# Fourth layer of a four-layer network on one core: retention in pieces beside the input products, outputs and gates by feature

## What is computed

```python
RET_HEADS, RET_DK, RET_DV = 4, 256, 512

def retention_mixer(h, w_in, w_out):
    proj = h @ w_in                                  # 1024 x 6144
    rq, rk, rv, rg = _split(proj, (1024, 1024, 2048, 2048))
    q = rotary(_heads(rq, RET_HEADS), pos)
    k = rotary(_heads(rk, RET_HEADS), pos) * RET_DK ** -0.5
    v = _heads(rv, RET_HEADS)
    o = retention_chunkwise(q, k, v)   # o_t = sum_{s<=t} gamma_h^(t-s) (q_t . k_s) v_s
    o = rms_norm_2(o) * jax.nn.silu(_heads(rg, RET_HEADS))
    return _merge(o) @ w_out                         # 2048 x 1024

x = x + gt_m * retention_mixer(rms_norm_2(x) * (1 + sc_m) + sh_m, ...)
x = x + gt_f * swiglu(rms_norm_2(x) * (1 + sc_f) + sh_f, ...)
```

## Time and profile before

| | before |
|---|---|
| median of 3 runs | 1613.58 us |
| the profiled execution | 1613.15 us |
| its span | 1611.4 us |
| PE, PE weight loads | 94%, 92% of the span |
| DVE, ACT, POOL | 67%, 47%, 26% |
| fourth layer's input products | 1190 to 1329.6 us |
| retention block, to the first output product | 1329.6 to 1359.9 us |

### The profile page before, as it was taken

How to read it: one execution, slowest core, us unless ns; L and a number is a source line. 1 busy time by engine, 2 the same in 40 slices (tenths; PEclk the granted TensorE clock), 3 DMA queues, 4 the chain that set the end, 5 groups by cost and what they waited for, 6 DMA issues and landing times. The chain is left out here.

```text
span 1611.4 us, 28191 instructions
## 1 busy us (share of the span) xinstructions
PE 1516.3 (94%) x12038; PEld 1485.3 (92%) x12038; DVE 1084.0 (67%) x1451; ACT 750.0 (47%) x1016; POOL 412.4 (26%) x395
## 2 busy tenths in 40 slices
PE   4999899998999999999997879999999997999998
PEld 4999899998998999998997869999999996999998
DVE  7878597796557497796766556776468754465544
ACT  3545465434646365434775234444354443354432
POOL 0123020693121020594001220200329502220022
PEclk9998799998999799998999979999989998999999
DMA  9773389795341469796441004877548771446550
GB/s 395 308 300 139 111 306 343 284 340 203 115 191 63 153 257 360 284 341 221 154 171 43 1 33 147 318 288 262 183 160 294 269 270 53 183 162 218 215 192 27
DMA packets 47212, 336.69 MB, mean 209 GB/s; under 512 B 5360, under 2 KB 5744, under 8 KB 6768
## 3 DMA queue, kind: packets, MB, share of 16 engines
q1 hardware_dynamic: 46224, 333.03, 55.5%
q10 hardware_dynamic: 864, 1.87, 0.3%
HBM read 333.83 MB, written 1.05 MB: 208 GB/s over the span
## 5 line engine op out<-in xcount | busy, mean ns | idle before, releaser
L432 DVE TENSOR_TENSOR weights_hi_lo<-ring,weights_hi_lo 128x1024 fp32r<-128x1024 f32 x426 | 552.3, 1319 | 302.9 <-ACT weights_hi_lo L425 301.8
L425 ACT ACTIVATE weights_hi_lo<-ring 128x1024 fp32r<-128x1024 f32 x426 | 444.4, 1058 | 501.5 <-PE PS L537 277.8
L537 PE MATMUL PS<-hi,weights_hi_lo 128*128 128x256 f32 x3200 | 522.5, 286 | 14.5 <-ACT hi L652 12.4
L537 PEld LDWEIGHTS PS<-hi,weights_hi_lo 128*128 128x128 f32 x3200 | 447.4, 194 | 17.9 <-issue 14.8
L836 PE MATMUL PS<-acts_hi_lo,weights_hi_lo 128*128 128x256 f32 x3264 | 396.4, 284 | 8.2 <-DVE weights_hi_lo L432 8.0
L836 PEld LDWEIGHTS PS<-acts_hi_lo,weights_hi_lo 128*128 128x128 f32 x3264 | 392.8, 191 | 9.3 <-issue 8.6
L763 POOL CAST acts_hi_lo<-arena 128x256 fp32r<-128x256 f32 x144 | 135.6, 942 | 835.7 <-PE PS L836 419.9
L537 PE MATMUL PS<-lo,weights_hi_lo 128*128 128x256 f32 x1600 | 324.7, 285 | 0.0
L443 DVE CUSTOM_DVE_ANT_0 ring<-ring,cond 128x1024 f32<-128x1024 f32 x192 | 253.6, 1359 | 0.0
L537 PEld LDWEIGHTS PS<-lo,weights_hi_lo 128*128 128x128 f32 x1600 | 251.4, 193 | 0.0
L537 PE MATMUL PS<-weights_hi_lo,hi 128*128 128x256 f32 x1248 | 203.5, 285 | 1.2 <-ACT hi L652 1.2
(11 more groups left out here) (349 smaller groups left out, 1117.9 us busy)
## 6 DMA issues: line engine op xcount, KB each, us to landing
ring<-in_stream_dram SPq DMA_DIRECT2D x313, 1024.0 KB, 4.9
constS<-in_const_dram SPq DMA_DIRECT2D x1, 1856.0 KB, 8.6
cond<-in_rows_dram SPq DMA_DIRECT2D x2, 512.0 KB, 5.2
arena<-in_x_dram ACTq DMA_DIRECT2D x1, 1024.0 KB, 11.3
smallS<-in_small_dram SPq DMA_DIRECT2D x1, 883.0 KB, 13.4
out_dram<-arena ACTq DMA_DIRECT2D x2, 256.0 KB, 2.5
out_dram<-arena SPq DMA_DIRECT2D x2, 256.0 KB, 3.3
constS<-in_const_dram SPq DMA_DIRECT2D x1, 320.0 KB, 14.7
```

The lines of the kernel that those rows point to most:

```text
L425: act.activation(wsp[:, g % 2, 0, at:at + HALF], ring[:, n % RING, at:at + HALF], ACT.Copy).then_inc(*ready.one())
L432: dve.tensor_tensor(wsp[:, g % 2, 1, at:at + HALF], ring[:, n % RING, at:at + HALF], wsp[:, g % 2, 0, at:at + HALF].bitcast(F32), ALU.subt ...
L537: mm = pe.matmul(o, lhs, rhs, start=k + g + j == 0, stop=k == KD - 1 and j == 2, skip_group_check=True)
```

## The change

The fourth layer's `ret_phase` and its block are gone. `retention` gives all four generators for `gemm_phase`: scores behind slots 10, 12, 13 and 15, head outputs behind 12, 14, 18 and 19, now by feature in pairs of banks (values stationary, decayed scores moving, four column blocks of 256 and 128 columns a head); squares on ACT, added in pairs on DVE, summed over the partitions by one-column products; root, reciprocal, spread over the partitions and copied to SBUF; DVE multiplies the outputs with it, and with the gates. The gates come by feature, through two buffers of 512 columns, so ACT's evacuation of slot i waits for DVE's gate of slot i - 2. The input products use three banks instead of four, and the first output slot is split in the same block (`split_weights`). The output products stand in the same block, and POOL's split waits for the gated pairs.

```diff
             before = state.pop("taken", None)
+            banks_free = state.pop("normed_heads", None)
...
+                if banks_free:
+                    pe.wait_ge(*banks_free)
                 for i, n in enumerate(slots):
...
             QK = area(0, 16, SEQ)
-            V, G = area(4096, TT, 2048), area(8192, TT, 2048)
-            oT = area(0, 16, SEQ)
+            V = area(4096, TT, 2048)
+            gates = area(TEMP_AT, 2, 512)
+            gated = sig("outputs_gated")
...
                     return act.activation(V[:, :, (i - 8) * 256:(i - 7) * 256], halves, ACT.Copy)
-                return act.activation(G[:, :, (i - 16) * 256:(i - 15) * 256], halves, ACT.Silu)
+                if i >= 18:
+
+                    act.wait_ge(*gated.at(i - 17))
+                return act.activation(gates[:, i % 2, :], bank, ACT.Silu)
+
             def proj(blk):
-                gemm_phase(blk, ("proj", l), lambda i: 0 if i < 8 else 256, evac, beside=(None, None, None, rotations(QK)))
-            return proj, lambda: ret_phase(QK, V, G, oT), oT
-
-        def rotations(QK):
+                gemm_phase(blk, ("proj", l), lambda i: 256 if 8 <= i < 16 else 0, evac, banks=3, split_weights=True,
+                           beside=retention(QK, V, gates))
+            return proj, None, QK
+
+        def retention(QK, V, gates):
...
+            att = later.rearrange("p (h k) -> p h k", h=4)
+            sq = area(TEMP_AT + 1024, 2, 512)
+            r = stat[:, 64:72]
+            yT = QK
+            taken, gated = sig("gemm_bank_taken"), sig("outputs_gated")
...
+            score_at, out_at = {10: 0, 12: 1, 13: 2, 15: 3}, {12: 0, 14: 1, 18: 2, 19: 3}
+            state["normed_heads"] = yn.at(8)
+            state["gated"] = [gated.at(i + 1) for i in range(8) for _ in range(2)]
+
+            def pair_banks(h):
+                return PS[:, 4 + h % 2 * 2:6 + h % 2 * 2, :].rearrange("p b (c t) -> p (b c) t", c=2)
...
+                    ins = pool.tensor_tensor(x2, t[2], t[0], ALU.add)
+                    ins.then_inc(*rot_done.one())
+                    pool.wait_ge(*rot_done.at(h + 1))
...
+            def pe_beside(pe):
+                for i in range(24):
+                    if i in score_at:
+                        h = score_at[i]
+                        pe.wait_ge(*rot_done.at(h + 5))
+                        if h:
+                            pe.wait_ge(*at_.at(h))
                         for kt in range(TT):
                             for c in range(2):
...
+                                mm = pe.matmul(PS[:, 3, 256 * kt:256 + P * kt], QK[:, 8 + 2 * h + c, kt * P:(kt + 1) * P],
                                                QK[:, 2 * h + c, kt * P:SEQ], start=c == 0, stop=c == 1)
                         mm.then_inc(*ap_.one())
...
+                    if i in out_at:
+                        h = out_at[i]
+                        pe.wait_ge(*at_.at(h + 1))
+                        pe.wait_ge(*taken.at(10 + 2 * h))
+                        if h >= 2:
+                            pe.wait_ge(*yn.at(2 * h - 2))
+                        o = pair_banks(h)
+                        for c in range(4):
+                            for kt in range(TT):
+                                mm = pe.matmul(o[:, c, kt * P:SEQ], V[:, kt, h * 512 + c * P:h * 512 + (c + 1) * P],
+                                               att[:, h, 256 * kt:256 + P * kt], start=kt == 0 and c % 2 == 0, stop=kt == 1,
+                                               skip_group_check=True)
                         mm.then_inc(*op.one())
...
+                    if i in (16, 21):
+                        g = 0 if i == 16 else 1
+                        pe.wait_ge(*at_.at(4))
+                        if g:
+                            pe.wait_ge(*yn.at(4))
+                        for h in (2 * g, 2 * g + 1):
+                            pe.wait_ge(*ad.at(h + 1))
+                            for m in range(TT):
+                                mm = pe.matmul(PS[:, 3, 2 * (h % 2) + m:2 * (h % 2) + m + 1], sq[:, h % 2, m * P:(m + 1) * P],
+                                               ones[:, 0:1], start=h % 2 + m == 0, stop=True, skip_group_check=True)
+                        mm.then_inc(*gsum.one())
+                    if i in (17, 22):
+                        g = 0 if i == 17 else 1
+                        pe.wait_ge(*grc.at(g + 1))
+                        for j in range(4):
+                            mm = pe.matmul(PS[:, 3, j * P:(j + 1) * P], r[:, 4 * g + j:4 * g + j + 1].to_broadcast((P, P)), ident,
+                                           start=j == 0, stop=True, skip_group_check=True)
+                        mm.then_inc(*gsp.one())
+                    yield
+
+            def act_beside(act):
+                for i in range(25):
+                    for h, at in ((0, 14), (1, 16), (2, 20), (3, 21)):
+                        if i == at:
+                            act.wait_ge(*op.at(h + 1))
+                            if h:
+                                act.wait_ge(*ad.at(h))
+                            if h >= 2:
+                                act.wait_ge(*yn.at(4))
+                            for b in range(2):
+                                act.activation(squares(h, b), pair_banks(h)[:, 2 * b:2 * b + 2, :], ACT.Square).then_inc(*gsq.one())
+                    if i in (17, 22):
+                        g = 0 if i == 17 else 1
+                        act.wait_ge(*gsum.at(g + 1))
+                        act.activation(r[:, 4 * g:4 * g + 4], PS[:, 3, 0:4], ACT.Sqrt, bias=cst("eps"), scale=1.0 / 512).then_inc(*grt.one())
+                    if i in (18, 23):
+                        act.wait_ge(*gsp.at(1 if i == 18 else 2))
+                        act.activation(sq[:, 0, :], PS[:, 3, :], ACT.Copy).then_inc(*rsb.one())
+                    yield
+
+            def squares(h, b):
+                v = spare[:, 768:1536] if b else area(TEMP_AT + 1024, 2, 512)[:, h % 2, :]
+                return (v[:, 0:512] if b else v).rearrange("p (c t) -> p c t", c=2)
+
+            def dve_beside(dve, order):
+                for i in range(28):
+                    for h, at in ((0, 11), (1, 13), (2, 14), (3, 16)):
+                        if i == at:
+                            dve.wait_ge(*ap_.at(h + 1))
+                            dve.tensor_tensor(att[:, h, :], PS[:, 3, 0:384], dec[:, h, :], ALU.mult).then_inc(*at_.one())
+                    for h, at in ((0, 14), (1, 16), (2, 20), (3, 21)):
+                        if i == at:
+                            a, b = squares(h, 0), squares(h, 1)
+                            dve.wait_ge(*gsq.at(2 * h + 2))
+                            order(dve.tensor_tensor(a, a, b, ALU.add))
+                            dve.tensor_tensor(a[:, 0, :], a[:, 0, :], a[:, 1, :], ALU.add).then_inc(*ad.one())
+                    if i in (17, 22):
+                        g = 0 if i == 17 else 1
+                        dve.wait_ge(*grt.at(g + 1))
+                        dve.reciprocal(r[:, 4 * g:4 * g + 4], r[:, 4 * g:4 * g + 4]).then_inc(*grc.one())
+                    if i in (18, 23):
+                        g = 0 if i == 18 else 1
+                        dve.wait_ge(*rsb.at(g + 1))
+                        dve.wait_ge(*ap_.at(4))
+                        for h in (2 * g, 2 * g + 1):
+                            for b in range(2):
+                                v = sq[:, 0, h % 2 * 256:h % 2 * 256 + 256].unsqueeze(1).broadcast_to((P, 2, SEQ))
+                                dve.tensor_tensor(yT[:, 4 * h + 2 * b:4 * h + 2 * b + 2, :], pair_banks(h)[:, 2 * b:2 * b + 2, :], v,
+                                                  ALU.mult).then_inc(*yn.one())
+                    n = i - 19
+                    if 0 <= n < 8:
+                        dve.wait_ge(*taken.at(17 + n))
+                        dve.wait_ge(*yn.at(n + 1))
+                        v = yT[:, 2 * n:2 * n + 2, :].rearrange("p k t -> p (k t)")
+                        dve.tensor_tensor(v, v, gates[:, n % 2, :], ALU.mult).then_inc(*gated.one())
+                    yield
+
+            return pe_beside, act_beside, dve_beside, pool_beside
...
-        for l in range(2, len(LAYERS)):
-            _, mixers, mixed = layers[l]
-            mixers()
-            with block() as blk:
-                outputs(blk, l, mixed)
-                ffn_phases(blk, l)
-                if l + 1 < len(LAYERS):
-                    layers[l + 1][0](blk)
-                else:
-                    final_phase(blk)
+        layers[2][1]()
+        with block() as blk:
+            outputs(blk, 2, layers[2][2])
+            ffn_phases(blk, 2)
+            layers[3][0](blk)
+            outputs(blk, 3, layers[3][2], acts_ready=state.pop("gated"))
+            ffn_phases(blk, 3)
+            final_phase(blk)
```

65 lines of the change are left out of this document (4 added, 61 removed).

## The result

The changed kernel ran at 1598.41 us, the median of four runs (1596.39 to 1601.72), against 1613.25 for the kernel before; the ratio is 0.9911 [0.9891, 0.993], 0.9% less. The forecast was 1602.1 with a range of 1599.0 to 1607.0: the direction and the mechanisms came out, and the time lies 0.6 us under the lower end.

The account below looks back on a forecast made before the run. PE, busy 94%, bounds the kernel; gains lie in the 30.3 us retention block. 30.3 - 19.7 of PE pieces - 1.6 wait = 9.0; + 2.7 clock - 0.6 table load = 11.1; 1613.15 - 11.1 = 1602.1 us, range 1599.0 to 1607.0.

Parts of the forecast that it names:

- two groups of sums: Sums of squares on PE beside the slots: two groups of four one-column products, 2 x 1.0 = 2.0 us.
- two spreads: Spreading the normalising factors on PE: two groups of four products, about 1.25 us each, 2.5 us.
- changes between kinds: Fourteen switches on PE between input products and retention pieces, bounds 0 and 0.1 us each, taken as 0.5 us.
- wait at the seam: PE's wait where the input products end and the output products begin, about 1.6 us.
- clock behind the seam: Clock 1.00 instead of 0.51 in the 5.5 us after the first output product starts, 2.7 us regained.
- table load in the norm: Norm after the output products must load the root's table because Silu's is in place, 0.6 us lost.
- rivals 2 and 4: Held splits stall PE beside the slots, 1604 to 1608 (chance 0.13); nothing to be measured, 1611.2 (chance 0.03).
- Room (a): Piece after slot 10: DVE's split half ready at 7.03 us, PE wants it at 7.06; room nil, once.
- The seam (c): After slot 22: chain over ACT and DVE of 8.5 us against PE's own 6.9, so PE waits about 1.6.
- Rival 3: Brief PE stops at pieces within the slots make the clock fall repeatedly, slower than before; seven falls 1617.5; chance 0.03.
- rival 5: More than forecast: seam hidden, norm's load hidden, no cost of changes; 13.8 us saved, 1599.3; chance 0.07.
- Rival 1: Clock falls at the seam all the same, costing 1.7, at most 2.7 us; 1603.8, up to 1605; chance 0.27.

Follow-up runs that it names:

- second execution: The kernel before the change run once more, untouched, for a second profile; 1610.14 us.
- the two additions: Changed kernel with two more additions of 512 on DVE before the first head's decay, behind slot 10; 1601.39 us (one run).
- pre-splitting: Kernel before with only the first output slot's weights split at the end of the input products, retention block kept; 1609.32 us, ratio 0.9978.

## Why the prediction was right or wrong

| term, us | forecast | shown |
|---|---|---|
| gap to the first output product | 30.3 | 30.3; 30.1 in the second execution |
| scores, four heads | 5.24 | 5.0 (1.23 to 1.31 each) |
| head outputs | 10.5 | 10.5, by doubling (10.2 from start to start, 2.54 each) |
| two groups of sums | 2.0 | 1.6 |
| two spreads | 2.5 | 1.6 |
| gates by feature | -1.0 | -1.0 (0.87 by undoing it) |
| changes between kinds | 0.5 | 0.5, what is left over (0.8 with the 10.2) |
| wait at the seam | 1.6 | 1.09 |
| **saved up to the output products** | **9.0** | **10.8** |
| clock behind the seam | +2.7 | +2.4 in the trace of record; 1.4 as a mean of four |
| table load in the norm | -0.6 | -0.6 behind the shortest sums; -0.5 as a mean |
| **sum** | **11.1** | 11.7 with the two means |

The 10.8 is 170.13 of the kernel before (second execution) less 159.36: both have 5.70 in slots 0 to 7 and 5.76 in slots 8 to 15. The 0.5 follows: 30.1 + 1.0 - 1.1 - 10.8 = 19.2 of PE's pieces, of which 18.7 are in the rows of the table. The prediction counted fourteen changes; the twelve pieces stand in eleven places, with 23 changes. The first group of a slot behind a piece takes 0.80 from start to start where the others take 0.70 to 0.72, which makes about 1 us in eleven places. The 1.4 is the mean of 47.93, 45.52, 47.03 and 47.06 less 45.52; the 0.5 is 7.55 less the mean of 6.42, 6.93, 7.85 and 6.94. Then 1613.25 - 11.7 = 1601.6, and the ten executions have their median at 1599.9: the sum is good to 2 us. Where the rest lies is not shown. From the up phase behind the norm to the end the ten changed traces took 194.5 to 196.5 us and the four of before 195.2 to 197.1, in code that is the same.

**Right.** The block's waits and transposes go, PE pays for its pieces in full, and no piece stalls it, so rivals 2 and 4 did not happen. Room (a), next to nil, was shown by the two additions. The seam (c) was shown by taking it away. The load in the norm was shown by leaving Silu out. The Trainium skill, ScalarE: Activation LUTs, section What ACT_TABLE_LOAD costs, adds a drain of about 1.38 us, and this case's traces do not agree: the root starts 0.01 us behind the load's end, and the load 0.02 behind the end of the instruction before it. Rival 3 did not happen: the twelve pieces between the slots left the clock at 1.00 through the 95 us of the stretches shown. The section A second HAM failure mode: psum-queue depth-cycling of the Trainium skill's page TensorE: Matmul & The Clock Gate does not describe these slots; its condition, frequent small idles, did not arise, since PE never stopped at a piece.

**Wrong, in two steps.** First, three terms were sized too dear, 1.8 us in all. The spreads: "four rows take 0.71, eight about 1.25"; eight take 0.80 from start to start. The row's 0.71 (and 1.05 now) is a duration with its tail, and the tail lies under the next product; a group's price is the distance to the next start. The sums the same way: 1.0 a group from the norm's 0.123 a row, 0.81 shown. The seam's chain of 8.5 was 0.7 too long and PE's own 6.9 0.15, so the wait of 1.6 was 0.5 too long. Against this the clock term was too rich: 2.7 was taken from the one trace with the deepest fall, and four traces give 1.4. That the sum of 11.1 stands so near 11.7 is in part luck.

Second, and this decides it, **the range** under "Numbers": "for 8 in 10 the range runs from rival 5's 1599.3, a little under". It held only mechanisms of the change. It gave no term to executions of one and the same kernel, which the runs show to lie 10 us apart (changed kernel 1596.39 to 1606.23, kernel before 1607.57 to 1619.15 in 34 runs), so that a median of four can stand 2 us from that of ten: 1598.41 against 1599.90. The mis-sized terms alone do not explain it: rival 5 with the shown terms is 11.7 + 1.1 + 0.5 + 0.8 = 14.1, or 1599.1, still over 1598.41. That the four runs fell under the range, and the next six (1601.42) did not, is luck of the draw. Three sources of the spread can be seen in unchanged code. The first input product of this layer started anywhere from 1186.18 to 1194.33 in the fourteen traces; a pace step of 0.064 us a slot is 0.5 us in eight slots; and each fall of the clock at the output products costs 1.3 to 2.4.

Rival 1 is settled for the wait that there is: six traces with 1.03 to 1.09 us, none with a fall. It was a fair rival for a wait of 2 us: with 2.5 the clock fell both times. What it took from the earlier trace rows was right for that length only: the forecast wait of 1.6 lay among the six stops of 1.30 to 1.81 us that had kept the clock.

**Open:** what sets the pace of a phase in an execution, and why one stop of 3.61 us kept the clock. Neither was tried. Nor was it tried whether pre-splitting made the transposes slower.

## What to carry to other kernels

Price a small group of matmuls put between others by the distance from its start to the next start, not by its rows' duration. Work that is moved beside a saturated PE is paid in full, so count what goes: here waits of 4.3 and 3.9 us, transposes, boundaries, and the clock that the waits had cost. Look for the half-clock work behind each long wait too: the 32 transposes behind the wait of 4.3 us ran at a mean clock of 0.68 in three traces and 0.55 in the fourth, where they took 1.2 us more and ate most of the 1.5 that a shorter wait behind them gave.

Before giving a range, look how far apart runs of one kernel lie, and add that to the mechanisms.

## What the hardware showed that was not expected

- The same product stream ran at one of three paces in an execution, 5.63, 5.70 or 5.76 us a slot with the weights still, at clock 1.00, and kept it through slots 0 to 7; with the activations still it was 5.76 in every trace. The gates' slots, with the weights still again, ran at 5.63 in every trace of the changed kernel that has them so.
- At two places the granted clock behind a stop went with the stop's length: 1.00 behind all 12 stops of 1.03 to 1.81 us, 0.51 to 0.73 behind 14 of the 15 of 1.90 to 4.71. The length of the last stop alone does not tell it elsewhere: behind the norm ahead of the fourth layer, a stop of 1.21 us at 1190.07 in the kernel before was followed by a clock of 0.50 until 1194, but there PE had stood still more than once just before.
- The norm's four spreading products took 1.22 us in 13 of 14 traces and 0.71 in the earlier trace rows: that execution, the one on record, had the quicker norm by 0.5 us.
